# A transformer layer on one core: how a few expert weight chunks are cut into DMAs, mid-stream and at the end

## The chip, the cores and the metric

One core of a Trainium2 chip runs the whole program. The metric is the device time of one execution in microseconds (us).

## What is computed

One layer of a streaming encoder on 512 tokens of 1024 channels, in float32: a token mixer (attention and retention), a cross-attention, and a mixture of experts, then a last RMSNorm. Only the experts matter here. A router picks 4 of 32 experts for each token; each expert is

```
hc = xb @ w1[e] + b1[e]                  # w1[e] 1024 x 2048
act = silu-like(hc[:, :1024]) * (clip(hc[:, 1024:]) + 1)
yb = act @ w2[e] + b2[e]                 # w2[e] 1024 x 1024
out[token] += gate * yb                  # the token's four experts
```

All 32 experts' weights, 12 MB for each, are read from HBM once.

## The kernel before

Five engines run written-out programs of their own and meet at semaphores: SP issues the weight loads, PE multiplies, ACT and DVE copy and apply the activation, GpSimd (POOL) gathers and scatters token rows.

Up to about 736 us of the span the core works on the token mixer, the cross-attention and the routing. From then on it goes through the experts, in an order by their number of tokens (expert n here is the n-th in that order). An expert's weights are 12 **chunks** of 1 MB: 8 of the first layer (W1, `w_exp_in`) and 4 of the second (W2, `w_exp_out`). A chunk is a tile of 128 partitions ("rows") of 8 KB each. The chunks go into a ring of 15 slots (SLOTS); slots 12 to 14 lie in the tile `moe`, so their loads show as `moe<-in_w_exp_in`. There are 384 chunks (CHUNKS).

SP's program (from line 477): after the first 15 loads, `refill` (line 504) waits until PE has used the chunk that was in the slot (`w_used`) and issues one DMA of all 128 rows through `load` (lines 486 and 487), which adds 16 to the slot's semaphore `w_ring`. The order of refills is PE's order of use: the 8 first-layer chunks of expert n+1, then the 4 second-layer chunks of expert n. Six turns of a loop (line 514) handle five experts each (TURN = 5). The very last chunk (number 383, lines 524 to 531) is loaded in eight DMAs instead: rows cut into runs of 2, 4, 6, 8, 10, 12 and 14, each with a semaphore of its own (`w_edge`), and then the 72 rows that are left, on `w_ring`.

PE's program (from line 1877): `up` (line 1885) multiplies an expert's first layer, waiting in `chunk_in` for each chunk before 4 matmuls for each group of 32 tokens (line 1903; experts have 3, 3, 2 groups in turn). `down` (line 1910) does the same for the second layer with 8 matmuls a group (line 1927). The order is up(n+1), down(n). `last_down` (line 1932) is the second layer of the last expert: it waits for the seven `w_edge` semaphores and for `w_ring` before the last chunk's matmuls (line 1954).

After each `down`, ACT copies the result (line 971) and sends it to HBM with four DMAs (line 978): to `y_main`, and for the last expert but one to `y_late`. When chunk 379, the last of `down` of the last expert but one, has landed (line 655), POOL gathers the tokens' rows of `y_main` by indirect DMAs of 128 rows of 4 KB (line 662), eight at once and further ones as DVE has added the earlier ones (line 1516). It gathers from `y_late` (line 667) when those stores have landed (line 672). PE adds the last rows (line 1974), then come the norm and the stores of the output (line 545).

Of the kernel before, what the change touches and what calls it, by code (L numbers as in the profile page):

```python
# [22 lines left out]
P = 128  # L23
# [36 lines left out]
EC = W1 + W2  # L60
SLOTS = EC + 3
CHUNKS = NE * EC
TURN = 5
SILU_MAX = float(np.float32(ALPHA * LIMIT / (1.0 + np.exp(-ALPHA * LIMIT))))
PAIRS = HEADS // 2
UNITS = [(p, kb) for p in range(PAIRS) for kb in (3, 2, 1, 0)]
# [29 lines left out]
def up_chunk(n, c):  # L96

    return n * EC + c - (W2 if n else 0)


def down_chunk(n, q):

    return (n + 1) * EC + (W2 if n < NE - 1 else -W2) + q


def loads_of(slot):

    return len(range(slot, CHUNKS, SLOTS))
# [56 lines left out]
def layer_kernel(nc, x, mem, g_mix, w_in, w_sb_o, w_ret_o, w_mix_out, g_xattn, g_mem, w_cq, w_ckv, w_co,  # L165
# [4 lines left out]
    DP = 2 * DENSE  # L170
# [7 lines left out]
    with ExitStack() as ctx:  # L178
# [3 lines left out]
        def sem(name):  # L182
            return ctx.enter_context(nc.semaphore(name))
# [132 lines left out]
        def m_(a, n):  # L316
            return moe[:, a:a + n]
# [3 lines left out]
        def x_t(g):  # L321
            return m_(1024, KT * 32 * g).rearrange("p (k n) -> p k n", k=KT)
# [13 lines left out]
        def held(s):  # L336
            return ring[:, s, :] if s < EC else m_(5120 + CH * (s - EC), CH)
# [21 lines left out]

        w_landed = [sem(f"w_landed{n}") for n in range(RAW)]  # L360
        w_ring = [sem(f"w_ring{n}") for n in range(SLOTS)]
        w_edge = [sem(f"w_edge{n}") for n in range(7)]
        w_hi, w_lo, w_used = sem("w_hi"), sem("w_lo"), sem("w_used")
        in_x = [sem(f"in_x{t}") for t in range(TT)]
        in_mats, in_cols, in_rot, in_mem, in_res = (
# [38 lines left out]
        def dense_source(g):  # L404

            for s in slabs.values():
                if s.chunk0 <= g < s.chunk0 + s.chunks:
                    break
            half, name = g - s.chunk0, s.name
            order = list(slabs)  # L410
            if order.index(name) < 13:
                src, col = w_in[0], order.index(name)
            else:
                src = {"so": w_sb_o, "ro": w_ret_o, "mo": w_mix_out, "mk": w_ckv, "mv": w_ckv,
                       "cq": w_cq, "co": w_co}[name[:2]][0]
                col = int(name[2]) + (2 if name[:2] == "mv" else 0)
            return src[half * 512:(half + 1) * 512, col * 512:(col + 1) * 512].rearrange("(a p) n -> p a n", p=P)

        def expert_chunk(e, c):
            if c < W1:  # L420
                return w_exp_in[0, bass.ds(e, 1), c * P:(c + 1) * P, :].rearrange("o p n -> p (o n)")
            q = c - W1
            return w_exp_out[0, bass.ds(e, 1), 2 * P * q:2 * P * q + 2 * P, :].rearrange("o (p a) n -> p (o a n)", a=2)
# [52 lines left out]
        @block.sync  # L476
        def _(sp):
            for t in range(TT):
                sp.dma_start(x_nat[:, t, :], x[0, t * P:(t + 1) * P, :]).then_inc(in_x[t], 16)
            for g in range(DENSE):  # L480
                if g >= RAW:
                    sp.wait_ge(w_lo, 2 * (g - RAW + 1))
                sp.dma_start(raw[:, g % RAW, :].rearrange("p (a n) -> p a n", a=4),
                             dense_source(g)).then_inc(w_landed[g % RAW], 16)

            def load(e, c, s):
                sp.dma_start(held(s), expert_chunk(e, c)).then_inc(w_ring[s], 16)  # L487

            for s in range(SLOTS):
                if s == 0:  # L490
                    sp.wait_ge(w_used, 2 * (slabs["mv1"].chunk0 + slabs["mv1"].chunks))
                elif 2 <= s < 6:
                    sp.wait_ge(w_lo, 2 * (DENSE - RAW + s - 1))
                elif s == 6:
                    sp.wait_ge(w_used, DP)
                elif s == EC + 1:
                    sp.wait_ge(b_hi, 3)
                    sp.wait_ge(b_lo, 2)
                load(s // W1, s % W1, s)

            def expert_at(n):
                return sp.value_load(order[0:1, bass.ds(n, 1)], min_val=0, max_val=NE - 1)

            def refill(e, c, k, turn=0):

                sp.wait_ge(w_used, turn + (DP + k - SLOTS + 1))
                load(e, c, k % SLOTS)

            for c in range(SLOTS - W1, W1):
                refill(1, c, up_chunk(1, c))  # L510
            for q in range(W2):
                refill(0, W1 + q, down_chunk(0, q))
            sp.wait_ge(order_ready, 1)
            with sp.Fori(0, (NE - 2) // TURN) as m:
                some = [expert_at(m * TURN + (1 + i)) for i in range(TURN + 1)]
                for i in range(TURN):
                    for c in range(W1):
                        refill(some[i + 1], c, up_chunk(2 + i, c), m * (TURN * EC))
                    for q in range(W2):
                        refill(some[i], W1 + q, down_chunk(1 + i, q), m * (TURN * EC))  # L520
            final = expert_at(NE - 1)
            for q in range(W2 - 1):
                refill(final, W1 + q, down_chunk(NE - 1, q))
            sp.wait_ge(w_used, DP + CHUNKS - SLOTS)
            row = 0
            for n, landed in zip((2, 4, 6, 8, 10, 12, 14), w_edge):
                rows = slice(row, row + n)
                sp.dma_start(held((CHUNKS - 1) % SLOTS)[rows, :], expert_chunk(final, EC - 1)[rows, :]).then_inc(landed, 16)
                row += n
            rows = slice(row, P)  # L530
            sp.dma_start(held((CHUNKS - 1) % SLOTS)[rows, :], expert_chunk(final, EC - 1)[rows, :]).then_inc(w_ring[(CHUNKS - 1) % SLOTS], 16)

            sp.wait_ge(route_done, 2)
            n = sp.value_load(n_over, min_val=0, max_val=OVER)
            with sp.If(n > 0):
                with sp.Fori(0, OVER) as j:
                    with sp.If(j < n):
                        b = sp.value_load(table[0:1, bass.ds(j, 1)], min_val=0, max_val=OB - 1)
                        sp.wait_ge(w_used, j * EC + (DP + NE * EC))
                        for c in range(EC):  # L540
                            load(b % NE, c, c)

            for tt in range(TT):
                sp.wait_ge(f_last, tt + 1)
                sp.dma_start(out[0, tt * P:(tt + 1) * P, :], o_sb[:, tt, :]).then_inc(stored[tt % 2], 16)
            sp.wait_ge(stored[0], 32)
            sp.wait_ge(stored[1], 32)
# [502 lines left out]
        def _(dve):  # L1050
# [427 lines left out]
            def swiglu(n, g, up_end, first=False):  # L1478
# [7 lines left out]
                dve.wait_ge(s_ready, n + 1)  # L1486
                nc.vector.scalar_tensor_tensor(act_n[:, 0:g], glu_s[:, 0:g], SILU_MAX, act_n[:, 0:g], ALU.min, ALU.mult).then_inc(act_ready, 1)

# [91 lines left out]
        def _(pe):  # L1580
# [296 lines left out]
            def chunk_in(k, over=None, c=None):  # L1877

                if over is None:
                    pe.wait_ge(w_ring[k % SLOTS], 16 * (k // SLOTS + 1))  # L1880
                    return held(k % SLOTS)
                pe.wait_ge(w_ring[c], over * 16 + 16 * (loads_of(c) + 1))
                return held(c)

            def up(n, g, sel, first=False, over=None):

                pe.wait_ge(xt_kept, n + 1)
                if not first:
                    pe.wait_ge(s_ready, n)
                    pe.wait_ge(lin_ready, n)  # L1890
                pe.wait_ge(sel_ready, sel)
                for j in range(g):
                    for s in range(4):
                        ins = nc.tensor.matmul(ps[32 * s:32 * s + 32, j, :], sel_now, b_in[:, s, :, :], start=True, stop=False,
                                               tile_position=(0, 32 * s), skip_group_check=True)
                if first:
                    ins.then_inc(sel_used, 1)
                xt = x_t(g)
                for k in range(KT):
                    w = chunk_in(None if over is not None else up_chunk(n, k), over, k).rearrange("p (g s n) -> p s g n", g=2, s=4)  # L1900
                    for j in range(g):
                        for s in range(4):
                            ins = nc.tensor.matmul(ps[32 * s:32 * s + 32, j, :], xt[:, k, 32 * j:32 * j + 32], w[:, s, :, :],  # L1903
                                                   start=False, stop=(k == KT - 1), tile_position=(0, 32 * s), skip_group_check=True)
                    ins.then_inc(w_used, 1)
# [127 lines left out]
            n = pe.value_load(n_over, min_val=0, max_val=OVER)  # L2033
# [45 lines left out]
```

## Time and profile before

| | us |
|---|---|
| three runs | 1822.68, 1822.80, 1826.49 |
| their median | 1822.8 |
| the profiled execution's own time | 1823.05 |
| its span, first to last instruction | 1821.3 |
| PE busy | 1716.2 (94% of the span) |
| experts' part of the span | about 736 to 1821 |

The experts' part is 1085 us long, and in it the 16 DMA engines are busy nearly all the time: the page's slices show 361 to 414 GB/s from about 730 us to the last slices but two. A busy PE doesn't tell what it is limited by; the waits in front of its instructions do.

### The profile page before, as it was taken

The page shows a single profiled execution, that of the slowest core. Times are in us where ns is not written, and L with a number is a line of the kernel's source. Part 1 is how long each engine was busy: PE and PEld are TensorE (multiplying, and loading weights), DVE is VectorE, ACT ScalarE, POOL GpSimd, SP SyncE. Part 2 cuts the span into 40 slices and gives each one's busy share as a digit, 9 for nine tenths or more (in the row PEclk, how much of TensorE's full clock was granted, in tenths as well). Part 3 has the DMA queues.
Part 4 walks back from the last instruction along what each step waited for, and adds up shares of the span by engine and source line. Part 5 has one row for each costly group of instructions (what it writes and reads, how often), then busy time and mean ns, then how long its engine had stood idle before and what let it go on. Part 6 is the DMA issues. An engine that isn't in the chain of part 4 may idle for free.

```text
span 1821.3 us, 36224 instructions
## 1 busy us (share of the span) xinstructions
PE 1716.2 (94%) x15650; PEld 949.4 (52%) x15650; DVE 451.3 (25%) x846; ACT 385.8 (21%) x602; POOL 101.5 (6%) x185
## 2 busy tenths in 40 slices
PE   7999999999999998999999999999999999998976
PEld 5766687788788766334343434333333343343322
DVE  4354426325545345700010101010000000000005
ACT  5454233324334325001000000000000010010001
POOL 0010000000000020000000000000000000000013
PEclk9999999999999999999999999999999999999998
DMA  7202231224225333999999999999999999999997
GB/s 237 70 24 82 84 101 46 70 93 161 93 79 199 116 93 146 364 390 378 407 398 407 401 404 401 407 409 398 411 402 403 410 401 407 410 397 409 408 328 261
DMA packets 105765, 505.74 MB, mean 278 GB/s; under 512 B 10565, under 2 KB 21333, under 8 KB 56373
## 3 DMA queue, kind: packets, MB, share of 16 engines
q1 hardware_dynamic: 83956, 461.40, 64.5%
q0 software_dynamic: 8352, 29.01, 5.2%
q10 hardware_dynamic: 13312, 13.12, 2.1%
q8 instruction: 126, 2.06, 0.5%
q14 instruction: 19, 0.15, 0.0%
HBM read 488.28 MB, written 15.20 MB: 276 GB/s over the span
## 4 chain that ended last, share of the span: by engine, by line
PE 57%; SPq 22%; DMA 13%; DVE 3%; issue 2%; ACT 2%; POOL 0%; ACTq 0%; POOLq 0%; DVEq 0%
SPq L487 21%; PE ps L1903 14%; PE ps L1583 9%; PE ps L1585 9%; PE ps L1584 9%; DMA ring<-in_w_exp_in 7%; PE ps L1927 6%; DMA ring<-in_w_exp_out 5%; PE ps L1680 1%; PE ps L1735 1%; PE ps L1754 1%; DMA work<-y_main,work 1%; PE ps L1974 1%; PE ps L469 1%; PE ps L1624 1%
## 5 line engine op out<-in xcount | busy, mean ns | idle before, releaser
L1903 PE MATMUL ps<-ring,moe 128*32 128x512 f32 x4408 | 490.3, 594 | 26.7 <-DMA ring<-in_w_exp_in 26.5
L1903 PEld LDWEIGHTS ps<-ring,moe 128*32 128x32 f32 x4408 | 130.4, 110 | 369.8 <-issue 265.9
L1483 DVE TENSOR_SCALAR moe<-ps 128x768 f32<-128x768 f32 (+1 forms) x32 | 28.0, 875 | 885.2 <-PE ps L1903 885.2
L1927 PE MATMUL ps<-ring,moe 128*32 128x256 f32 x4320 | 240.0, 379 | 6.3 <-DMA ring<-in_w_exp_out 5.8
L1057 DVE TENSOR_TENSOR wl<-raw,wh 128x1024 fp32r<-128x1024 f32 x104 | 126.2, 1224 | 259.6 <-ACT wh L718 259.6
L1927 PEld LDWEIGHTS ps<-ring,moe 128*32 128x32 f32 x4320 | 129.3, 110 | 106.9 <-DMA ring<-in_w_exp_out 10.0
L718 ACT ACTIVATE wh<-raw 128x1024 fp32r<-128x1024 f32 x104 | 108.9, 1057 | 255.9 <-PE ps L1585 255.2
L1583 PE MATMUL ps<-oph,wh 128*128 128x512 f32 x384 | 151.1, 393 | 2.4 <-DVE work L1190 1.6
L958 ACT ACTIVATE moe<-ps 128x768 f32<-128x768 f32 (+1 forms) x32 | 23.8, 744 | 599.6 <-DVE moe L1483 599.6
L1584 PE MATMUL ps<-opl,wh 128*128 128x512 f32 x384 | 150.0, 391 | 0.0
L1585 PE MATMUL ps<-oph,wl 128*128 128x512 f32 x384 | 149.9, 390 | 0.0
L1903 PE MATMUL ps<-moe 128*32 128x512 f32 x1096 | 124.1, 594 | 7.9 <-DMA moe<-in_w_exp_in 7.8
L1583 PE MATMUL ps<-wh,oph 128*128 128x512 f32 x288 | 114.4, 397 | 3.8 <-DVE opl L1228 3.0
L1584 PE MATMUL ps<-wl,oph 128*128 128x512 f32 x288 | 112.6, 391 | 0.0
L1585 PE MATMUL ps<-wh,opl 128*128 128x512 f32 x288 | 112.6, 391 | 0.0
L1583 PEld LDWEIGHTS ps<-oph,wh 128*128 128x128 f32 x384 | 72.5, 189 | 19.3 <-issue 3.6
L1903 PEld LDWEIGHTS ps<-moe 128*32 128x32 f32 x1096 | 32.1, 110 | 94.0 <-issue 67.0
L1585 PEld LDWEIGHTS ps<-oph,wl 128*128 128x128 f32 x384 | 72.4, 188 | 15.3
L1584 PEld LDWEIGHTS ps<-opl,wh 128*128 128x128 f32 x384 | 72.4, 189 | 14.6
L618 POOL CAST sel_c<-work 96x32 bf16 (+1 forms) x64 | 17.1, 293 | 935.1 <-DVE moe L1337 906.4
L1583 PEld LDWEIGHTS ps<-wh,oph 128*128 128x128 f32 x288 | 54.5, 189 | 17.6 <-issue 4.7
L1585 PEld LDWEIGHTS ps<-wh,opl 128*128 128x128 f32 x288 | 54.4, 189 | 11.5
(303 smaller groups left out, 1534.7 us busy)
## 6 DMA issues: line engine op xcount, KB each, us to landing
ring<-in_w_exp_in SPq DMA_DIRECT2D x205, 1024.0 KB, 29.1
ring<-in_w_exp_out SPq DMA_DIRECT2D x103, 1024.0 KB, 28.5
moe<-in_w_exp_in SPq DMA_DIRECT2D x51, 1024.0 KB
raw<-in_w_in SPq DMA_DIRECT2D x26, 1024.0 KB, 5.1
moe<-in_w_exp_out SPq DMA_DIRECT2D x24, 1024.0 KB
raw<-in_w_ckv SPq DMA_DIRECT2D x8, 1024.0 KB, 5.1
y_main<-moe ACTq DMA_DIRECT2D x84, 96.0 KB
raw<-in_w_ret_o SPq DMA_DIRECT2D x4, 1024.0 KB, 5.0
```

What stands on the lines that cost most here:

```text
L469: ins = nc.tensor.matmul(ps[:, 6 + dt, :], v_x[:, m, a:a + P], prob_t[:, hd % 2, m * T:(m + 1) * T], start=(m == 0), stop=(m == MT - 1))
L487: sp.dma_start(held(s), expert_chunk(e, c)).then_inc(w_ring[s], 16)
L718: nc.scalar.activation(wh[:, slot, :], raw[:, c % RAW, g % 2 * PC:(g % 2 + 1) * PC], ACT.Copy).then_inc(w_hi, 1)
L958: nc.scalar.activation(glu_s[:, 0:g], ps[:, 0:g, 0:256].rearrange("p j (n a) -> p j a n", a=2), ACT.Silu, scale=ALPHA).then_inc(s_ready, 1)
L1057: nc.vector.tensor_tensor(wl[:, slot, :], raw[:, g // 2 % RAW, g % 2 * PC:(g % 2 + 1) * PC], wh[:, slot, :], ALU.subtract).then_inc(w_lo, 1)
L1483: nc.vector.tensor_scalar(act_n[:, 0:g], ps[:, 0:g, 256:512].rearrange("p j (n a) -> p j a n", a=2), 1.0 - LIMIT, 1.0 + LIMIT, ALU.max, AL ...
L1583: nc.tensor.matmul(o, a_hi_, b_hi_, start=start, stop=False)
L1584: nc.tensor.matmul(o, a_hi_, b_lo_, start=False, stop=False)
L1585: return nc.tensor.matmul(o, a_lo_, b_hi_, start=False, stop=stop)
L1624: ins = nc.tensor.transpose(ps[:, 4 + k % 4, t * P:(t + 1) * P], src[:, t, k * P:(k + 1) * P], ident)
L1903: ins = nc.tensor.matmul(ps[32 * s:32 * s + 32, j, :], xt[:, k, 32 * j:32 * j + 32], w[:, s, :, :], start=False, stop=(k == KT - 1), tile_ ...
L1927: ins = nc.tensor.matmul(y_bank(s, j), at[:, a, j, q, :], w[:, a, s, :], start=False, stop=(q == W2 - 1 and a == 1), tile_position=(0, 32 ...
```

## The change

First, in each turn of SP's loop, two of the 40 first-layer chunks (chunk 0 of the experts i = 1 and i = 3 of the five) are loaded by `refill_sides` in five DMAs: four of four rows each (rows 112 to 115, 116 to 119, 120 to 123, 124 to 127) on a semaphore `w_side`, then rows 0 to 111 in one DMA on `w_ring`. That is 12 chunks in all. PE waits for `w_side` (4 times 16) ahead of such a chunk.

Second, the last chunk of all is cut into 5, 7, 9, 11, 13 and 15 rows and then 68 rows, in place of 2, 4, 6, 8, 10, 12, 14 and 72: seven DMAs in place of eight.

```diff
+EDGES = (5, 7, 9, 11, 13, 15)
...
-        w_edge = [sem(f"w_edge{n}") for n in range(7)]
+        w_side = [sem(f"w_side{n}") for n in range(2)]
+        w_edge = [sem(f"w_edge{n}") for n in range(len(EDGES))]
...
+            def refill_sides(e, c, k, turn, landed):
+
+                sp.wait_ge(w_used, turn + (DP + k - SLOTS + 1))
+                w = expert_chunk(e, c)
+                for r in range(112, P, 4):
+                    sp.dma_start(held(k % SLOTS)[r:r + 4, :], w[r:r + 4, :]).then_inc(landed, 16)
+                sp.dma_start(held(k % SLOTS)[0:112, :], w[0:112, :]).then_inc(w_ring[k % SLOTS], 16)
...
                     for c in range(W1):
-                        refill(some[i + 1], c, up_chunk(2 + i, c), m * (TURN * EC))
+                        if c == 0 and i in (1, 3):
+                            refill_sides(some[i + 1], c, up_chunk(2 + i, c), m * (TURN * EC), w_side[i // 2])
+                        else:
+                            refill(some[i + 1], c, up_chunk(2 + i, c), m * (TURN * EC))
...
-            for n, landed in zip((2, 4, 6, 8, 10, 12, 14), w_edge):
+            for n, landed in zip(EDGES, w_edge):
...
                 for k in range(KT):
+                    if over is None and k == 0 and n >= 2 and (n - 2) % TURN in (1, 3):
+                        pe.wait_ge(w_side[(n - 2) % TURN // 2], 64 * ((n - 2) // TURN + 1))
```

## Rows read from the trace of the kernel before

**Rows 1.** The page: span, what bounds the chain that ended last, DMA packets.

```profile
span 1821.3 us, 36224 instructions
SPq L487 21%; PE ps L1903 14%; PE ps L1583 9%; PE ps L1585 9%; PE ps L1584 9%; DMA ring<-in_w_exp_in 7%; PE ps L1927 6%; DMA ring<-in_w_exp_out 5%; PE ps L1680 1%; PE ps L1735 1%; PE ps L1754 1%; DMA work<-y_main,work 1%; PE ps L1974 1%; PE ps L469 1%; PE ps L1624 1%
DMA packets 105765, 505.74 MB, mean 278 GB/s; under 512 B 10565, under 2 KB 21333, under 8 KB 56373
```

**Rows 2.** Stretches of the experts' part; last columns: granted PE clock, DMA share, GB/s.

```profile
736.00:866.00 130.00, 128.13 (x1528) 49.14 (x1532) 39.46 (x103) 10.88 (x17) 6.84 (x13) 0.99 0.98 375
960.00:1060.00 100.00, 100.00 (x1236) 39.15 (x1232) 6.95 (x12) 8.68 (x14) 4.44 (x9) 1.00 1.02 404
1060.00:1160.00 100.00, 97.33 (x1228) 39.13 (x1224) 8.51 (x16) 9.98 (x16) 4.67 (x11) 1.00 1.02 404
1560.00:1660.00 100.00, 92.69 (x1144) 36.26 (x1148) 6.95 (x12) 8.68 (x14) 3.69 (x9) 1.00 1.02 405
```

**Rows 3.** What PE waited for ahead of line 1903: 736 to 1060, then 1060 to 1756.

```profile
  issue: 141.9, 456
...
  DMA ring<-in_w_exp_in: 125.2, 142
```

**Rows 4.** Line 487, SP's loads to landing, issued at 742-866, 866-1000 and 1100-1300.

```profile
DMA to landing us min/median/max: 6.4/7.0/8.1
...
DMA to landing us min/median/max: 10.7/16.2/22.7
...
DMA to landing us min/median/max: 28.5/29.8/30.9
```

**Rows 5.** Short stretches at the end of the weight stream; columns as in rows 2.

```profile
1748.00:1752.00 4.00, 2.98 (x28) 0.83 (x32) 0.00 (x0) 0.00 (x0) 0.00 (x0) 1.00 1.02 426
1755.00:1758.00 3.00, 1.62 (x24) 0.65 (x16) 1.60 (x4) 1.08 (x2) 0.00 (x0) 1.00 0.97 197
1758.00:1761.00 3.00, 2.14 (x40) 1.33 (x44) 1.49 (x8) 0.00 (x0) 0.00 (x0) 1.00 0.71 164
1761.00:1764.00 3.00, 2.50 (x50) 1.29 (x44) 0.00 (x0) 0.00 (x0) 0.00 (x0) 1.00 0.51 194
1764.00:1767.00 3.00, 3.00 (x64) 1.79 (x60) 0.00 (x0) 0.00 (x0) 0.00 (x0) 1.00 0.52 216
1782.00:1787.00 5.00, 3.25 (x32) 0.69 (x24) 1.50 (x2) 0.00 (x0) 0.94 (x1) 1.00 1.01 367
```

**Rows 6.** SP's issue instructions: line 487 at 1100 to 1300, then lines 528 and 531.

```profile
L487 SPq DMA_DIRECT2D ring<-in_w_exp_in x40: 332/1940/7667, 1104.7 to 1292.1; - x40
...
L528 SPq DMA_DIRECT2D ring<-in_w_exp_out x7: 258/316/2277, 1745.8 to 1751.4; - x7
...
L531 SPq DMA_DIRECT2D ring<-in_w_exp_out x1: 544/544/544, 1751.9 to 1751.9; - x1
```

**Rows 7.** The chain of waits in order of time, from 1740 on.

```profile
1736.18 30.91 DMA ring<-in_w_exp_out
1769.90 16.80 DMA work<-y_main,work
1788.27 1.82 POOL work L662
1791.79 7.83 DMA moe<-y_late,work
1799.76 14.10 PE ps L1974 x32
```

**Rows 8.** The timeline at the end: PE's last chunks and ACT's copy.

```profile
1775.89 0.39 ACT L971 ACTIVATE moe<-ps 128x256 f32<-128x256 f32 x1 [18.41 <-remote]
1778.38 6.87 PE L1954 MATMUL ps<-ring,moe 128*32 128x512 f32 x48
1787.04 1.92 PE L1954 MATMUL ps<-ring,moe 128*32 128x512 f32 x16 [1.80 <-DMA ring<-in_w_exp_out]
```

**Rows 9.** DMA issues: ACT's store of token rows, last column us to landing.

```profile
h_rows<-work ACTq DMA_DIRECT2D x4, 512.0 KB, 12.5
```

## The prediction

> **What bounds the kernel.** I read the chain of waits first, then the stretches, then the end in order of time. The chain's largest entries in the experts' part are SP's issue of the loads (21%), line 1903 and landings of the ring (7% and 5%) [rows 1]: PE and the weight stream share the path, and one must ask when each leads. Up to 1060 us PE is never held up by a load: ahead of line 1903 only issue gaps stand [rows 3]. Yet the DMA engines are already full, at a share of 1.02 and 404 GB/s in 960 to 1060 [rows 2], and the time from a load's issue to its landing climbs from 7.0 over 16.2 to 29.8 us [rows 4]: the ring's 15 chunks of lead are being eaten. From 1060 on PE waits 142 times, 125.2 us, for first-layer chunks [rows 3] (the weight loads of PE and its matmuls each count such a wait, so the sum counts some twice), and its busy share falls to 92.69 of 100 us, while the DMA rate stays at 405 GB/s [rows 2]. So from about 866 us on the stream runs without a pause, and its pace sets the end.
>
> The reader should look longest at the end of the stream. The last load is issued at 1751.9 [rows 6], and until about 1768 nothing else is on the queues. Were the 16 engines alike, they would run out together. Instead the share (above 1 where packets overlap) falls from 1.02 to 0.71 and then stays at 0.51 and 0.52 [rows 5], while the last chunk reaches PE only at 1787.04, after a wait [rows 8]. So about half the engines have done everything, the last chunk included, near 1759 (0.97 and 0.71 over three us each are 4.1 us of the second half's work after 1755), and the other half is far behind. A chunk counts as landed when its last part has, so the **late half** sets the pace. The rate says what kind of limit that is: 405 GB/s over 16 engines is 25.3 GB/s for each; 216 GB/s over the 8 still working is 27.0. Had the total been the limit, eight alone would have sped up much more.
>
> **Price of a row.** Packets of 8 KB or more number 105765 - 56373 = 49392 [rows 1], and 384 chunks of 128 rows are 49152: a row is one packet, and an even split gives each engine 8 rows a chunk. One row costs its engine 8.192/25.3 = 0.324 us in the stream, 0.303 us at the rate of the late half alone.
>
> **Part one, the sides.** I take it that the 112 rows are split evenly over all 16 engines, 7 each, and that each four-row DMA puts its rows on the same four engines. No row shows which engine carries what, so this is the assumption to test. Then in each of the 12 chunks twelve engines carry 7 rows and four carry 11. The first such chunk (expert 3) is issued near 790, where landings take 7.0 us and the engines keep up, so it gives nothing; 11 count. If the late half lies among the twelve, it is relieved of 11 x 0.324 = **3.6 us** (bounds: 10 x 0.303 = 3.0 and 12 x 0.324 = 3.9). PE waits throughout, so all of this moves the end. If the small DMAs are spread evenly after all, the gain is 0; if one of the four is of the late half, it carries 3 rows more in each of some 10 chunks, 10 x 3 x 0.324 = 9.7 us lost. I take the first: the present cut of the last chunk already gives the first engines the most rows, 13 (one of each small run, six of the 72), and half of all engines are done by 1759 even so; late engines with 13 rows on top would be likelier to land after 1787 than at it.
>
> SP issues 48 DMAs more. Each takes 0.33 us when the queue has room and 1.94 us at the median when it is full [rows 6], so up to 4 x 1.94 = 7.8 us more on SP for a chunk. Behind them stand the 112-row DMA and all later loads, but the queue holds 29.8 us of work there [rows 4], so the engines don't run dry: nothing, and up to 7.8 us for a chunk were the backlog gone. In the first turn, where it is 7.0 us, an issue takes 0.33 us, 1.3 us in all, against a ring that is 15 chunks ahead. POOL's and ACT's queues are not moved past anything.
>
> The Trainium skill, "DMA: Bandwidth & Descriptors", Rules for kernel authors, speaks against this: cut transfers serialize on the same 16 engines, and small ones are mostly overhead, by its fit 2.0 us each. If these stood on the path the change would cost 48 x 2.0 = 96 us by it; the backlog above is why I leave that out.
>
> PE's new wait stands ahead of the chunk's 8 to 12 matmuls and everything after them. The four small DMAs are issued before the 112 rows of the same chunk, for which PE waits anyway, so it costs nothing unless the four engines become the last.
>
> **Part two, the end.** With runs of 2 to 14 rows and 72, cut one row to an engine from the first engine on, and 72 rows six each on twelve, late engines hold up to 11 rows of the last chunk; with 5 to 15 and the rest on four engines, at most 6 on any but those four. So the worst late engine has 5 rows fewer, 5 x 0.324 = 1.6 us (at the rate of 1782 to 1787, 367/16 = 22.9 GB/s, it is 1.8). Two paths feel it. PE stood idle 1.80 us for this chunk [rows 8]; and POOL's gather issued at 1769.90 landed after 16.80 us, in the same engines behind the same rows, and held back POOL's next ones [rows 7]. POOL then gathers from y_late at 1791.79, and PE's last 32 matmuls follow. What is late next is the store into y_late: ACT issues it right after its copy at 1775.89, near 1777.3; its nearest row, ACT's other row stores, lands in 12.5 us [rows 9], at 1789.8, so POOL can gain 2.0 us before that floor. I take **1.6 us**; bounds 0 and 2.0.
>
> On the four engines, the extra is 10 x 3 rows in the stream (9.7 us) and some 10 rows at the end (3.0 us): done at 1759 before, now at 1771.7, and up to 4 us later with POOL's gathers between, 1775.7. PE asks for the last chunk at 1778.38 + 6.87 - 3.6 = 1781.6. Margin 5.9 us, so nothing.
>
> ACT's copy at 1775.89 comes 5.8 us after PE's last matmul for it, for a cause the profile calls remote [rows 8]; I let it shift with the rest.
>
> Sum: -3.6 - 1.6 = -5.2 us against the profiled execution's 1823.05 (span 1821.3), so 1817.85; the median of the runs is 0.25 lower, so **1817.6**.
>
> **Rivals.** *The four engines become last* (0.18). The 68-row DMA may hang on four engines, 17 rows each; with the 6 of the small runs that is 23 rows, 7 us. If their lead is smaller than I read from one execution, the last chunk waits for them: the 1.6 is gone and up to 3.2 us of rows (10 x 0.324) come back. Stream gain 3.6 less half of that: -2.0, 1820.8. For it: the 12.7 us of new load against a lead of some 20. Against: the margin above. The Trainium skill has the rule ("DMA: Bandwidth & Descriptors", Why a DMA increments its semaphore by 16 and not by 1): a DMA from SP uses the largest number of engines up to 16 that divides its rows, the lowest-numbered ones. By it, 112 rows use all 16, four rows the first four, and 68 rows the same four; no view here can show it.
>
> *No half is relieved* (0.10): the small runs are spread over all engines, or the two halves trade places from time to time. 0 from the stream, 0 to -1.6 from the end: 1822.0. Against it: 216 GB/s from exactly half the engines.
>
> *The small DMAs fall on a late engine* (0.10), the slower case. The place is rows 112 to 127 of the 12 chunks, the price 9.7 us less what the end gives, up to 3 more with 10 extra rows there: 1822.8 + 9.7 = 1832.5. It decides from the first full chunk, near 866, and from the point where one of the four has no lead. For it: no row names engines.
>
> **How the numbers follow.** Forecast 0.62, with its own bounds -3.0 to -8 (3.9 + 2.0, and up to 2 more if ACT's remote wait shrinks too). A change of 0.2%, 3.6 us, is about what a measurement here can tell from none. Faster: 0.57 of the forecast and 0.05 of the first rival, 0.62. Same: 0.05 + 0.13 + 0.08 = 0.26. Slower: 0.10 + 0.02 = 0.12. The range of 1814.5 to 1823.0 leaves out the slow case and a few hundredths on the fast side.
>
> **What would show it.** Right: the stretch in which the share is near 0.5 after the last load shrinks, with a step between (four engines later than the other early ones); chunk 379 lands near 1763.5 where it was 1736.18 + 30.91 = 1767.1 [rows 7], and POOL's first gather follows; line 1954 shows no DMA wait; the y_late gather starts near 1786.6. PE's total wait for chunks falls by 3 to 4 us. Wrong: a share of 1.0 up to the last chunk with PE waiting on it (first rival); chunk 379 at 1767 as before (second); PE's waits larger from about 1000 us on, or waits on the sides (third).

## The result and the profile after

The changed kernel takes 1899.22 us (median of 4 runs, 1896.1 to 1902.32) against 1823.1 us: the ratio is 1.0411, with a 95% interval of 1.0393 to 1.0428. It is 76 us slower. The forecast was 1817.6, the range up to 1823.0, so even the slow rival's 1832.5 was far short.

The stretches of the experts' part, those of [rows 2] first (the last three columns are PE's granted clock, the DMA share and GB/s):

```profile
736.00:866.00 130.00, 127.48 (x1523) 50.12 (x1526) 40.06 (x104) 10.83 (x16) 6.82 (x13) 0.99 0.98 372
960.00:1060.00 100.00, 97.06 (x1184) 38.40 (x1180) 6.95 (x12) 9.48 (x15) 4.43 (x9) 0.98 1.02 358
1060.00:1160.00 100.00, 90.76 (x1128) 35.78 (x1124) 6.95 (x12) 8.04 (x14) 4.43 (x9) 1.00 1.02 383
1560.00:1660.00 100.00, 87.86 (x1084) 34.71 (x1080) 6.95 (x12) 8.67 (x14) 4.43 (x9) 1.00 1.02 375
```

The DMA share is 1.02 as before, but the engines now move 358 to 383 GB/s where they moved 404 and 405 [rows 2]. They are as busy and carry less: packets take longer. That is where the time went, all along the stream. A closer look around one of the 12 chunks, whose 112-row DMA is issued at 1199.9:

```profile
1200.00:1205.00 5.00, 3.69 (x36) 0.93 (x36) 0.00 (x0) 0.00 (x0) 0.00 (x0) 1.00 1.02 416
1210.00:1215.00 5.00, 5.00 (x51) 1.50 (x41) 0.10 (x1) 0.00 (x0) 0.00 (x0) 1.00 1.05 357
1215.00:1220.00 5.00, 4.62 (x87) 2.69 (x85) 2.43 (x4) 1.51 (x2) 1.33 (x3) 1.00 0.98 320
1220.00:1225.00 5.00, 2.19 (x40) 0.94 (x32) 0.00 (x0) 0.00 (x0) 0.00 (x0) 1.00 1.06 252
1225.00:1230.00 5.00, 3.83 (x38) 2.17 (x38) 0.00 (x0) 0.60 (x1) 0.00 (x0) 0.73 1.00 238
1235.00:1240.00 5.00, 5.00 (x52) 1.49 (x48) 0.00 (x0) 0.00 (x0) 0.00 (x0) 1.00 1.04 426
```

From 1210 to 1230 the rate falls to 238 GB/s with the engines busy, and then it is 426 again. The bytes missing against 405 GB/s in these four rows are 5 x (48 + 85 + 153 + 167) = 2265 KB, or 5.6 us of the stream. Twelve times 5.6 is 67 us. The small DMAs themselves cost SP little: their issue takes 0.31 us at the median, and no wait of PE is put down to one of them. Line 516 issues the four-row DMAs, line 517 the 112 rows:

```profile
L516 SPq DMA_DIRECT2D ring<-in_w_exp_in x48: 253/309/7665, 793.3 to 1736.0; - x48
...
L517 SPq DMA_DIRECT2D ring<-in_w_exp_in x12: 322/412/2119, 795.1 to 1736.5; - x12
```

PE waits for chunks of both layers now, with only 12 first-layer chunks changed. Its waits ahead of matmuls were 26.5 us in all for `ring<-in_w_exp_in` and 5.8 for `ring<-in_w_exp_out`:

```profile
PE ps L1918 <- DMA ring<-in_w_exp_in: 41.4, 52, 2.5
PE ps L1942 <- DMA ring<-in_w_exp_out: 36.1, 24, 3.1
```

The chain at the end, as in [rows 7] (line 675 is 662 of before, 1989 is 1974):

```profile
1807.11 30.93 DMA ring<-in_w_exp_out
1838.30 0.99 POOL work L675
1840.84 15.95 DMA work<-y_main,work
1862.16 7.76 DMA moe<-y_late,work
1870.06 16.88 PE ps L1989 x32
```

Chunk 379 lands and POOL's first gather starts at 1838.30, where it was 1767.36 (its gather at 1769.90 is the third): 70.9 of the span's 73.3 us are lost before that. From there to the y_late gather it is 23.9 us, and it was 24.4 (1791.79 - 1767.36). So the end gave about half a microsecond back, and PE's last matmuls took 2.8 us more.

### The profile page after: what moved, and what is told of

Its sections match the earlier page's. It is cut to its first block, busy times and chain, and to the rows that moved or that the text cites. A ratio compares the mean times of both kernels' runs of the same rounds, so it can differ in the third digit from the quotient of the medians.

```text
span 1894.6 us, 36376 instructions
## 1 busy us (share of the span) xinstructions
PE 1738.4 (92%) x15650; PEld 956.4 (50%) x15650; DVE 451.3 (24%) x846; ACT 385.7 (20%) x602; POOL 101.3 (5%) x185
## 4 chain that ended last, share of the span: by engine, by line
PE 53%; DMA 20%; SPq 19%; DVE 3%; issue 2%; ACT 2%; POOL 1%; ACTq 0%; POOLq 0%; DVEq 0%
SPq L489 18%; PE ps L1918 13%; PE ps L1596 9%; PE ps L1598 8%; PE ps L1597 8%; DMA ring<-in_w_exp_out 7%; DMA ring<-in_w_exp_in 7%; PE ps L1942 5%; DMA moe<-in_w_exp_in 3%; PE ps L1693 1%; PE ps L1748 1%; PE ps L1767 1%; PE ps L1989 1%; SPq L516 1%; DMA work<-y_main,work 1%
## 5 line engine op out<-in xcount | busy, mean ns | idle before, releaser
L1918 PEld LDWEIGHTS ps<-ring,moe 128*32 128x32 f32 x4408 | 132.3, 110 | 388.4 <-issue 263.8
L1942 PE MATMUL ps<-ring,moe 128*32 128x256 f32 x4320 | 253.4, 390 | 36.6 <-DMA ring<-in_w_exp_out 36.1
L1942 PEld LDWEIGHTS ps<-ring,moe 128*32 128x32 f32 x4320 | 132.7, 112 | 146.6 <-DMA ring<-in_w_exp_out 49.5
```

Of the source, the lines that this page charges most:

```text
L1942: ins = nc.tensor.matmul(y_bank(s, j), at[:, a, j, q, :], w[:, a, s, :], start=False, stop=(q == W2 - 1 and a == 1), tile_position=(0, 32 ...
```

## The experiments

Except in e2, the last chunk of all is cut as in the kernel before, or, where it is said, left whole. So each kernel is the one before with the change that is named. Where a chunk comes in several DMAs, all such chunks share one semaphore for what lands beside `w_ring`.

### Which part: e1_sides_only and e2_edges_only

```diff
-EDGES = (5, 7, 9, 11, 13, 15)
+EDGES = (2, 4, 6, 8, 10, 12, 14)      # e1, against the changed kernel
...
-            for n, landed in zip((2, 4, 6, 8, 10, 12, 14), w_edge):
+            for n, landed in zip((5, 7, 9, 11, 13, 15), w_edge):      # e2, against the kernel before
```

> The 12 chunks as 112 rows and four times four rows, the last chunk cut as before (one semaphore for all sides in place of two). Theory A (the 112-row DMA spoils the packets: each of the 16 engines no longer writes the partitions that it writes in a 128-row DMA, and the engines get in each other's way) and theory B (the small DMAs are dear in themselves) both put the loss of 76 us into the mid-stream chunks: 1885 to 1900 us. Theory C (the end of the stream, with 68 rows on four engines, is where it is lost): near 1820 us.

> The last chunk as 5, 7, 9, 11, 13, 15 and 68 rows, all other chunks as before. Theories A and B: the mid-stream is that of the kernel before, so within 4 us of 1823. My prediction's term for this part was 1.6 us faster, its bounds 0 and 2.0. Theory C: most of the 76 us, over 1870 us.

e1 took 1899.82 us (ratio 1.0429, 1.0404 to 1.0453), e2 1820.87 us (0.9989, 0.9980 to 0.9998). The sides carry the whole loss. The new cut of the last chunk gained 1.7 us by the medians beside it (1822.57), which the interval barely tells from nothing. Theory C fell. Two lines of e2's chain show the landing of chunk 379 and the y_late gather:

```profile
1736.15 33.56 DMA ring<-in_w_exp_out
1789.86 7.75 DMA moe<-y_late,work
```

### The small DMAs or the 112 rows: e3_112_alone and e4_small_extra

```diff
             def refill_sides(...):
-                for r in range(112, P, 4):
-                    sp.dma_start(held(k % SLOTS)[r:r + 4, :], ...)      # e3, against the changed kernel
...
-                    sp.dma_start(held(k % SLOTS)[r:r + 4, :], ...)
-                sp.dma_start(held(k % SLOTS)[0:112, :], ...)
+                    sp.dma_start(w_(0, CH)[r:r + 4, :], ...)            # e4, against the changed kernel
+                load(e, c, k % SLOTS)
```

> The 12 chunks load only their rows 0 to 111, in one DMA; rows 112 to 127 are left out (the slot keeps older data there), there are no small DMAs and PE waits for none. 1.5 MB less is read in all. Theory A: most of the loss stays, 1870 to 1895 us. Theory B: no loss, 1815 to 1823 us. Theory D (four engines with 11 rows of a chunk are too slow): no loss either, as every engine has 7 rows.

> The 12 chunks are loaded whole in one 128-row DMA as before; ahead of each, the four small DMAs of four rows still run, but write the same partitions of an idle buffer, so 1.5 MB more is read than in the kernel before and PE waits for them. Theory A: little, 1823 to 1840 us (four engines carry 4 rows more in each of 12 chunks, 48 x 0.324 = 15.6 us, less their lead). Theory B: 48 small DMAs cost what they did, 1885 to 1900 us. Theory D: more than the changed kernel's share of the rows, since the four engines have 12 rows a chunk here: over 1835 us and PE waiting for loads after each such chunk.

e3 took 1891.07 us (1.0381, 1.0360 to 1.0401), e4 1835.27 us (1.0074, 1.0056 to 1.0093), beside 1822.57. One DMA of 112 rows in place of 128, with nothing else and with fewer bytes, costs 68.5 us over 12 chunks, 5.7 us for each. Theories B and D fell by it: neither the number of small DMAs nor the load on four engines is needed for most of the loss (e4 alone, at 1835.27, would have fitted D's "over 1835 us"). The small ones do have a price, 12.7 us for 48. In e4 SP also waits once, ahead of its loop, until the idle buffer is free (`h_stored`); e9 below has the same wait and loses nothing. Here is the middle of the stream in e3, then in e4, over two stretches of 200 us:

```profile
1060.00:1260.00 200.00, 178.28 (x2137) 68.13 (x2141) 13.90 (x24) 15.66 (x25) 8.86 (x18) 0.99 1.02 379
1260.00:1460.00 200.00, 176.11 (x2128) 67.30 (x2124) 11.36 (x20) 16.05 (x26) 7.31 (x15) 0.99 1.02 374
```

```profile
1060.00:1260.00 200.00, 187.72 (x2308) 72.74 (x2300) 13.89 (x24) 17.34 (x28) 8.85 (x18) 1.00 1.02 399
1260.00:1460.00 200.00, 186.84 (x2296) 72.92 (x2288) 13.90 (x24) 17.34 (x28) 8.89 (x18) 1.00 1.02 400
```

The share is the same 1.02 in both, the rate 374 to 379 in the one and 399 to 400 in the other.

### What about 112 rows: e5_cols, e6_64_64, e7_source_shift, e8_quiet

```diff
-                sp.dma_start(held(k % SLOTS)[0:112, :], w[0:112, :])...
+                for h in range(2):      # e5: halves of every row
+                    sp.dma_start(held(k % SLOTS)[:, h * PC:(h + 1) * PC], w[:, h * PC:(h + 1) * PC])...
...
+                for h in range(2):      # e6: rows 0 to 63, rows 64 to 127
+                    sp.dma_start(held(k % SLOTS)[64 * h:64 * h + 64, :], w[64 * h:64 * h + 64, :])...
...
+                w = w_exp_in[0, bass.ds(e, 1), 3:3 + P, :]...      # e7
+                sp.dma_start(held(k % SLOTS), w)...
...
-                load(s // W1, s % W1, s)
+                if s == 2:      # e8, in the first fill; s == 3, 4, 5: 120, 96 and 64 rows
+                    sp.dma_start(held(s)[0:112, :], expert_chunk(0, s)[0:112, :])...
```

> The 12 chunks in two DMAs of all 128 rows each, the left and the right half of every row (4 KB packets, twice as many). Theory A1 (what costs is that a DMA of other than 128 rows makes the engines write partitions outside their own groups): all 16 engines keep their groups, so 1822 to 1832 us. Theory A2 (any second DMA for a chunk disturbs the stream, whatever its rows): half of the 76 us or more, over 1855 us.

> The 12 chunks in two DMAs of 64 rows each, 8 KB packets, 4 rows for each engine in each: the same bytes, packets and balance as in the kernel before. Theory A1: the engines leave their groups in part, so clearly slower, 1840 to 1890 us. Theory A3 (only a number of rows that gives each engine an odd or uneven share, as 7, is dear): 1823 us.

> The 12 chunks in one DMA of 128 rows into the same partitions as before, but the rows are read from 3 rows (24 KB) further on in the expert's weights, so those chunks hold rows that belong elsewhere. Theory A4 (the loss is on the HBM side: the engines' stretches of source no longer begin at the usual multiples): slower, 1850 us or more. Theory A1: only the destination counts, 1823 us.

> Four chunks of the first fill are loaded while the DMA engines do nothing else, as 112, 120, 96 and 64 rows, each alone; the rows that are left come later in DMAs of their own. A 128-row chunk alone lands 4.4 to 4.5 us after its issue, of which 8 rows at 0.31 us are 2.5. Theory A1, if the engines of one DMA already get in each other's way: 112 rows take longer than 128, 6 us or more, and so do 96 and 64 for their rows. If only a meeting with other transfers costs: 112 rows land after 4.2 us, 96 after 3.9, 64 after 3.3. 120 rows should take as long as 128 (eight rows on each of fewer engines) or longer. The time as a whole: within 3 us of the kernel before.

| | us | ratio to before, 95% interval |
|---|---|---|
| e5_cols | 1824.71 | 1.0006 (0.9995 to 1.0018) |
| e6_64_64 | 1916.73 | 1.0523 (1.0468 to 1.0579) |
| e7_source_shift | 1821.50 | 0.9994 (0.9980 to 1.0009) |
| e8_quiet | 1824.35, one run | beside 1823.27 |

Two DMAs for a chunk cost nothing if each spans all 128 partitions. A source that begins 3 rows further on costs nothing either. Two DMAs of 64 rows, with the bytes and the packets of the kernel before, cost 93 us, more than the change itself and above my range of 1840 to 1890. So neither an odd share for each engine (A3) nor a shifted start in HBM (A4) is the cause; which rows go together in a DMA is. A row and its partition go together in all of these kernels but e7, so that it is the writing and not the reading that suffers is argued, and not shown by itself.

e8 loads chunks one at a time, long before the stream. A 128-row chunk there lands 4.8 us after its issue (the load at 607.8 in the kernel before). The answers for 112, 120, 96 and 64 rows, in this order (lines 503, 505, 507 and 509 of e8_quiet):

```profile
DMA to landing us min/median/max: 5.6/5.6/5.6
...
DMA to landing us min/median/max: 7.1/7.1/7.1
...
DMA to landing us min/median/max: 6.9/6.9/6.9
...
DMA to landing us min/median/max: 6.3/6.3/6.3
```

Half the rows take 1.5 us longer than all of them. The 128-row figure was 4.8, not the 4.4 to 4.5 that I had written down, and my guess of 6 us or more for 112 rows was a little high. Only the DMAs of 112 and 120 rows were alone, though: beside those of 96 and 64 rows POOL's loads kept the engines busy for 43% and 34% of the time. The single packets in the traces settle what that leaves open. An 8 KB packet of the 128-row load at 607.8 took 0.31 us at the median, one of the 128-row load that the kernel before issues at 676.5, beside loads of POOL as well, 0.32, and one of the 64 rows 0.60. With 112 and 120 rows, alone, it was 0.43 and 0.59. So packets of one DMA hinder each other with no other traffic about, and up to 18 packets of the 64-row DMA were under way at once, as many as in the 128-row one: it isn't short of engines.

The Trainium skill has the map that fits this, "SBUF — State Buffer", Door 1: The DMA port swizzle. DMA traffic enters the partitions by 16 ports, each serving four partitions and the four that lie 32 further on; partitions 0 to 63 reach only 8 of them. By it, each 64-row DMA of e6 sends its rows through 8 ports, and a DMA of rows 0 to 111 gives 12 ports eight rows each and four ports four. The packets of twice the time in e8's 64-row DMA agree; no run here tests that groups 32 apart share a port. The Trainium skill, "DMA: Bandwidth & Descriptors", Rules for kernel authors, says of two transfers to disjoint partition halves "Don't bother", because both use the same engines one after the other. e6 agrees with the advice, but queueing alone doesn't give its 93 us: e12 below has two transfers for a chunk too, and loses nothing.

### The map put to a test: e9_strided_extra and e12_even_odd

```diff
-                    sp.dma_start(w_(0, CH)[r:r + 4, :], w[r:r + 4, :])...
+                    sp.dma_start(w_(0, CH)[32 + r:48:4, :], w[32 + r:48:4, :])...      # e9, against e4
...
-                    sp.dma_start(held(k % SLOTS)[64 * h:64 * h + 64, :], w[64 * h:64 * h + 64, :])...
+                    sp.dma_start(held(k % SLOTS)[h::2, :], w[h::2, :])...              # e12, against e6
```

> As e4_small_extra (whole 128-row chunks, four extra four-row DMAs ahead of each of the 12), but each small DMA writes partitions 32, 36, 40, 44 (then 33, 37, ...), one in each of four neighbouring groups of four, in place of four in one group. Theory P (what is scarce is the way into a group of partitions; two engines that write the same group at once each run at half rate): the four engines of a small DMA no longer write one group at once, so less than e4's 12.7 us: 1824 to 1832 us. If only the extra rows on four engines cost: the same 1835 us.

> The 12 chunks in two DMAs of 64 rows as in e6_64_64, but the even rows and then the odd rows, so each DMA writes to all groups of partitions, four rows in each pair of groups, and not to one half of them. Theory P: no group is loaded more than another, so far less than e6's 93 us: under 1850 us. Theory A1 in its plain form (each engine must write its own rows of the 128-row split, or it costs): as e6, over 1890 us.

e9 took 1824.39 us (0.9999, 0.9990 to 1.0009) and e12 1825.12 us (1.0000, 0.9990 to 1.0010), beside 1824.48. Both losses are gone, 12.7 us of e4 and 93 us of e6, with the same numbers of DMAs, rows and bytes. e9 changed two things, though: its four rows lie in four groups, and they lie in partitions 32 to 47 in place of 112 to 127; that the place doesn't matter was not tried. This is e6, then e12, over the same stretches:

```profile
1060.00:1260.00 200.00, 170.76 (x2020) 65.10 (x2012) 11.36 (x20) 16.05 (x26) 7.33 (x15) 0.98 1.02 370
1260.00:1460.00 200.00, 174.44 (x2098) 69.22 (x2098) 12.32 (x21) 14.87 (x25) 7.55 (x15) 0.99 1.01 366
```

```profile
1060.00:1260.00 200.00, 192.37 (x2378) 75.33 (x2373) 14.58 (x25) 17.86 (x30) 8.88 (x18) 1.00 1.02 405
1260.00:1460.00 200.00, 189.11 (x2332) 74.40 (x2324) 14.57 (x26) 18.14 (x30) 8.91 (x18) 1.00 1.02 405
```

The single packets say the same. Of SP's 8 KB packets that start between 866 and 1740, these took over 0.45 us (the median is 0.31 in each of them):

| | packets over 0.45 us | the run's loss |
|---|---|---|
| before | 1251 | |
| e12, e9, e17 | 1135, 1245, 1168 | none |
| e16 | 1565 | 6 us |
| e15, e4 | 1858, 1956 | 17 and 12.7 us |
| the changed kernel, e3, e6 | 4305, 4570, 5361 | 76, 68.5 and 93 us |

In e3 the 112-row DMAs of that stretch have at most 11 x 112 = 1232 packets, and there are 3319 slow ones more than before. So at least 2000 of them belong to DMAs that the change leaves alone.

The plain form of A1, that an engine must write the groups it writes in a 128-row DMA, isn't settled. e12 was to refute it, but no view shows which engine writes which row, and e12's stripes may leave each engine in its own groups. What is shown is that a DMA whose rows are a block slows the stream, and that stripes that touch every group of four alike don't. e9 also shows that 48 more DMAs and 1.5 MB more cost nothing that can be measured.

### Does each one count: e10_six_chunks

```diff
-                        if c == 0 and i in (1, 3):
+                        if c == 0 and i == 1:      # against e3
```

> As e3_112_alone (rows 112 to 127 left out, one DMA of 112 rows), in 6 of the 12 chunks. If each such DMA disturbs the stream by itself (theories A1 and P): half of e3's 68.5 us, 1850 to 1862 us. If the first ones only tip the engines out of step for the rest of the stream (theory S): 1875 to 1895 us, nearly all of it.

1848.18 us (1.0132, 1.0114 to 1.0151), 23.7 us over the 1824.48 beside it and just under the range for A1 and P. The disturbances pass (theory S fell), as the 426 GB/s at 1235 above shows. But six cost 4.0 us each and twelve 5.7 each; why the other six are dearer was not tried.

### The end: e11_whole_last

```diff
-            for n, landed in zip((2, 4, 6, 8, 10, 12, 14), w_edge):
-                ...
-            rows = slice(row, P)
+            rows = slice(0, P)
```

> The last chunk of all in one DMA of 128 rows, no cut. My prediction took the present cut (2 to 14 and 72 rows) to matter by the rows that a late engine holds, 8 here against up to 11: by that the end comes 3 x 0.324 = 1.0 us earlier than in the kernel before. Theory P: the 72 rows are a cut of the bad kind, and without it the packets of the end run at full rate, so 1 to 4 us faster than before.

1820.43 us (0.9972, 0.9959 to 0.9984): 4.1 us by the medians beside it, 5.1 by the ratio. The upper end of theory P's 1 to 4 us was right, the count of rows (1.0 us) too small. In the kernel before, the rate was 197 and 164 GB/s at shares of 0.97 and 0.71 [rows 5]. In e11:

```profile
1755.00:1758.00 3.00, 2.42 (x25) 0.48 (x18) 0.00 (x0) 0.00 (x0) 0.00 (x0) 1.00 0.95 396
1758.00:1761.00 3.00, 3.00 (x57) 1.89 (x60) 2.19 (x6) 1.09 (x2) 0.00 (x0) 1.00 0.54 221
1764.00:1767.00 3.00, 3.00 (x60) 1.68 (x56) 0.00 (x0) 0.00 (x0) 0.73 (x1) 1.00 0.51 210
```

The quotient of the rate and 16 times the share, what a busy engine moves, is 12.7 and 14.4 GB/s there and 26.1 and 25.6 in e11's first two rows. From 1752 to 1764, 177 of 306 of SP's 8 KB packets took over 0.45 us before, and 1 of 456 in e11. So the present cut of the last chunk is itself of the bad kind, and the fastest kernel of this study is the one before with its last chunk uncut. Which of that cut's eight DMAs does it was not tried. In e11 PE no longer waits for that chunk. What holds it is ACT's copy, 9.7 us after the last `down` matmul:

```profile
1779.21 0.38 ACT L966 ACTIVATE moe<-ps 128x256 f32<-128x256 f32 x1 [19.32 <-remote]
```

It is the instruction of [rows 8], 5.8 us after that matmul before. Its cause the profile doesn't show, and I made no run for it.

### Is the idea good in a good form: e13 to e17

```diff
             def refill_sides(...):      # e13; e15 has the first two lines as one DMA of [7::8]
+                for r in range(7, P, 32):
+                    sp.dma_start(held(k % SLOTS)[r:r + 25:8, :], w[r:r + 25:8, :])...
+                sp.dma_start(held(k % SLOTS)[0::2, :], w[0::2, :])...
+                sp.dma_start(held(k % SLOTS)[1::4, :], w[1::4, :])...
+                sp.dma_start(held(k % SLOTS)[3::8, :], w[3::8, :])...
...
             def refill_sides(...):      # e16, 6 chunks; e17 has the first two lines as one DMA of [3::4]
+                for r in range(3, P, 16):
+                    sp.dma_start(held(k % SLOTS)[r:r + 13:4, :], w[r:r + 13:4, :])...
+                sp.dma_start(held(k % SLOTS)[0::2, :], w[0::2, :])...
+                sp.dma_start(held(k % SLOTS)[1::4, :], w[1::4, :])...
```

> The sides again, in a form that spreads each DMA over all groups: in the 12 chunks the rows 7, 15, 23, ... (16 rows) go in four DMAs of four rows, the other 112 as the even rows (64), every fourth from 1 (32) and every eighth from 3 (16), so twelve engines should carry 7 rows and four 11 as my prediction had it; the last chunk is cut as before. My prediction's term: 3.6 us faster than the kernel before, PE's waits for loads down by 3 to 4 us. Theory P (the way into a group of partitions is the scarce thing, and moving a row to another engine frees no way): no gain, 1822 to 1830 us.

> e13_clean_sides and the last chunk in one whole DMA (e11_whole_last) together. If both gains are real they add: 1822.8 - 5.1 - 3.6 = 1814 us. Theory P: e11's gain alone, near 1819 us or a little above.

> The cut of e13_clean_sides with no row moved to another engine: the 12 chunks as the even rows (64), every fourth from 1 (32), every eighth from 3 (16) and every eighth from 7 (16), each DMA on all 16 engines, 8 rows for each engine in sum. If e13's 20.9 us come from moving the 16 rows onto four engines: 1823 to 1827 us. If they come from the 16-row DMAs, whose rows lie in half of the groups each: 1835 to 1845 us, and e13 says nothing on the idea of moving rows.

| | us | ratio to before, 95% interval |
|---|---|---|
| e13_clean_sides | 1843.96 | 1.0107 (1.0088 to 1.0125) |
| e14_clean_whole | 1834.28 | 1.0054 (1.0036 to 1.0071) |
| e15_same_cut_even | 1840.49 | 1.0088 (1.0054 to 1.0121) |

Neither of my two expectations for e13 held: 21 us slower, though I had thought its DMAs even. They aren't. Rows 3, 11, 19 and so on lie in every second group of four. e15, which moves nothing, loses 17 us with the same cut, so e13 says nothing on the idea. e14, the same with the last chunk whole, missed both of its figures too, for the same reason. It is 9.7 us faster than e13, more than twice e11's 4.1; why was not tried. In the last pair the larger DMAs touch every group alike, and each DMA of four rows has one row in each of four groups:

> As many rows moved as in the changed kernel (192), in DMAs that are all even over the groups of partitions: in 6 chunks, rows 3, 7, 11, ... (32 rows) go as eight four-row DMAs (rows 3, 7, 11, 15, then 19, ...), the other 96 as the even rows and every fourth from 1. Twelve engines should carry 6 rows and four 14 in such a chunk. If late engines are limited by their own packets (my first term): 6 x 2 x 0.324 = 3.9 us faster than e17_not_moved. If the way into the partitions is the limit (theory P): no gain against e17, or slower.

> The same cut in the same 6 chunks with the 32 rows in one DMA on 16 engines: nothing moved. All its DMAs write to all groups evenly, so by theory P within 2 us of the kernel before, as e12_even_odd; if 32-row DMAs are dear in themselves, 5 us or more slower.

e17 took 1824.15 us (0.9998, 0.9988 to 1.0007), e16 1830.24 us (1.0032, 1.0021 to 1.0042), beside 1824.43. The cut is free, and loading 192 of its rows in four-row DMAs, which was to put them on four engines, costs 6 us where my term said 3.9 us gained. e16 over the two stretches, then e17:

```profile
1060.00:1260.00 200.00, 189.19 (x2328) 72.98 (x2324) 13.89 (x24) 17.37 (x28) 8.87 (x18) 1.00 1.02 402
1260.00:1460.00 200.00, 187.75 (x2316) 73.50 (x2312) 13.89 (x24) 17.37 (x28) 8.88 (x18) 1.00 1.02 403
```

```profile
1060.00:1260.00 200.00, 192.05 (x2379) 75.37 (x2375) 14.93 (x26) 18.39 (x30) 8.86 (x18) 1.00 1.02 405
1260.00:1460.00 200.00, 188.71 (x2328) 73.40 (x2324) 14.57 (x27) 17.59 (x29) 9.26 (x20) 1.00 1.02 406
```

## Why the prediction was wrong

**What bounds the kernel** held: from about 866 us on the stream runs without a pause and sets the end. It is why a loss in 12 of 384 chunks shows whole: 70.9 us before POOL's first gather.

**Price of a row** is the step that failed. The prediction wrote "One row costs its engine 8.192/25.3 = 0.324 us in the stream" and took that price for any row on any engine. It is the price in a stream of 128-row DMAs, the only kind of weight load before the last chunk. I divided bytes by engines and never asked whether it matters which rows go together in a DMA. In the changed kernel packets of the same size take longer, and those of other DMAs too: 238 GB/s at a DMA share of 1.00, and 4305 packets over 0.45 us where there were 1251. e3 puts 5.7 us on each 112-row DMA, e6 7.8 us (93/12) on each pair of 64 rows, e12 nothing on the same pair in stripes.

**The sides.** "If the late half lies among the twelve, it is relieved of 11 x 0.324 = 3.6 us" was wrong twice. The 112-row DMA costs 5.7 us for each chunk where 0.324 us was to be gained. And without that cost the relief didn't come: e16 against e17 is 6 us the wrong way. A reading that fits is that a row moved to another engine still has to enter the same group of partitions, so nothing is freed, and the engine that now writes there gets in the way of another: e16 has about 400 slow packets more than e17. That is argued. More rows on few engines isn't enough for the loss, since e9 has as many in four-row DMAs, on top of whole chunks, and loses nothing; why e16 does was not tried. The argument "216 GB/s over the 8 still working is 27.0" showed a limit for each engine or for what it writes to. I took the first; no row told them apart.

**SP's issues and PE's wait** held at nothing: e9 has 48 small DMAs more and PE's wait for them, and loses nothing. The estimate that I set aside, 48 x 2.0 = 96 us by the fit on the Trainium skill's page "DMA: Bandwidth & Descriptors", Anatomy of one DMA, stood near the measured 76, and was still wrong: e9 has the DMAs without the loss. The page gives that fit for DMAs that GpSimd issues, and these are SP's.

**The end.** The term was 1.6 us faster, and e2 measured 1.7. The size is right, the reason only half, and so it is partly luck. POOL's path gained: the y_late gather starts at 1789.86 in e2 and at 1791.79 before [rows 7]. PE's path did not: it waits up to 2.5 us at line 1954 where it waited 1.80 [rows 8] and was to wait for nothing. Chunk 379 landed later in e2, at 1769.7 where it was 1767.1; that the 68-row DMA loads the end as badly as the 72-row one fits, and was not tried by itself. e11 shows what the term missed, 4 to 5 us from no cut at all.

**The rivals.** None was it. *The small DMAs fall on a late engine* had the right sign and a price of 9.7 us against 76. Its sign, larger waits of PE from about 1000 us on, came true, and did not tell it from the true cause. What its own mechanism (more rows on four engines) costs isn't settled, 0 in e9 and 6 us in e16 for 192 rows each, but it isn't 76. Missing was a rival in which the changed DMA slows packets that it doesn't own. The profile of before has a hint: in [rows 5] the rate at 1758 to 1761 is 164 GB/s with a share of 0.71, that is 164/(16 x 0.71) = 14.4 GB/s for a busy engine, where 1764 to 1767 has 26.0. I read the share and passed over that quotient; it comes from the last chunk's cut, since e11 has 25.6 there. So after 1755 the early half had less work left than its share says.

## What to carry to other kernels

Where a stream of loads sets the time, cut a full-width load by columns or in stripes of rows that touch every group of four partitions alike (even and odd rows were free), not as a block of rows: 64 + 64 rows cost 7.8 us a pair here, 112 rows 5.7 us, and neighbouring transfers pay too. To see such a cost, divide the rate by 16 and by the DMA share: with 8 KB packets it was 25 to 27 GB/s in good stretches here and 12 to 15 where packets hindered each other (238 GB/s at a share of 1.00 is 14.9). A price per byte read from one shape of DMA holds for that shape alone.

## What the runs showed that I had not expected

- A DMA of 64 rows landed after 6.3 us and one of 96 after 6.9, beside some loads of POOL; alone, one of 112 rows took 5.6, one of 120 took 7.1 and one of 128 took 4.8. Packets of the 64 rows took 0.60 us, and of the 128 rows 0.31.
- Four rows in one group of four partitions, 48 times, cost 12.7 us in a full stream (e4); four rows in four groups, elsewhere in the partitions, cost nothing (e9).
- A count of rows for each group is not the full story. If 64 rows go through half of the ways, an estimate is that they take twice their time, some 2.6 us a chunk more at 0.324 us a row; e6 lost 7.8. The engines are at least 9 us apart at the end of the stream (the share is near 0.5 from about 1759 to 1768 [rows 5]), so one chunk's block meets other chunks' rows, and the slow packets of e3 are mostly theirs. Why the sum is so large was not tried.
